# Token mixing: the bias rows of decay and rate as a 65th row of the raising products

## The chip, the cores and the metric

One Trainium2 chip, one of its NeuronCores. The metric is the device time of one execution in microseconds (us), lower is better. TensorE multiplies, VectorE (DVE), ScalarE (ACT) and GpSimd (POOL) do the rest, SyncE (SP) issues most transfers.

## The reference, cut to what matters

The program is a chain of layers over 256 tokens of width 2048. The change lies in the first of them, in the token mixing (an RWKV-7 recurrence with 16 heads of 64). Of its 288 narrow columns the first 64 raise the decay, the next 64 the rate `a`, the last 160 the gate:

```
r, k, v, zw, za, zg = _split(z, RW_SPLITS)          # ..., 64, 64, 160 columns
w_log = -jax.nn.softplus(-(w0 + jnp.tanh(zw) @ w_decay_up).astype(f32)) - 0.5
decay = jnp.exp(-jnp.exp(w_log))
a = jax.nn.sigmoid((a0 + za @ w_icl_up).astype(f32))
g = jax.nn.sigmoid(zg) @ w_gate_up
```

`w_decay_up` and `w_icl_up` are 64 x 1024, `w_gate_up` is 160 x 1024, `w0` and `a0` are rows of 1024. After this come the recurrence over the tokens, an attention branch, an expert layer and two more layers, which the change doesn't touch.

## The kernel before, in words

All weights come as one stream of units of 128 x 2048 values (1 MB). A unit lands in one of four slots (`ring`), ACT writes its rounded part (`hi_w`, lines 216 and 217), DVE the rest (`lo_w`, lines 222 and 224), and TensorE multiplies: line 635 (`quarter`) issues six products of 128 x 512 for a quarter of a unit, 24 for a unit. SP loads the unit four ahead when TensorE has finished one.

Everything else in this stage is laid by hand between the quarters of that stream. The token mixing is done in four pieces `n` = 0 to 3 (two halves of 512 columns, `hf`, times two tiles of 128 tokens, `i`), and `due(u, g, o)` says at which unit `u` and quarter `g` a step of a piece stands: piece `n` begins at unit 35.25 + 12 `n`, and step `o` stands `o` units later. Every engine walks the same table in its own order, and semaphores hold them together. For one piece:

- `ups` (o = 0, lines 775 to 778): the raising of decay and rate. Line 775 multiplies a row of ones (partition 32 of `zgT2`) by the row `w0` (partition 32 of `gup2`), line 776 adds the product of `zT[0:64]` (turned columns of the decay) and `up[0:64]`; lines 777 and 778 do it for the rate with partition 64 and partitions 64 to 127. They are plain float32, and each such product is two instructions on TensorE in the trace.
- `sigmoids` (ACT, lines 1104 and 1105) turn both banks into `sg` and `aa`, `rates` (DVE) uses `aa`.
- `sums` (o = 1, lines 789 to 793): three products of `sg` with masks of 128 x 128, and eight tiny ones.
- then `turns`, `levels`, a solve on DVE with round trips through DRAM, `first`, `second` (line 855), `third`, `states` and `reads`, up to o = 11.25, and `chain` (lines 907 and 916) for four chunks at o = 11.5, 11.75, 12 and 12.25. `inflow` (lines 880 and 881) follows in the first three of them. Piece `n` + 1 thus does its `ups` right behind chunk 2 of piece `n`, then comes one quarter of the stream, then chunk 3.

In chunk 0 of pieces 0 and 2 the state is zero; line 913 then closes the sum with a row of zeros (`zgT2[32:33, 1]`) times `gup2[32:33]`. `gates_up` (lines 834 and 835) raises the gate: 128 rows, and the tail of 32 rows at partitions 0 to 31 of `zgT2` and `gup2`.

`turn_z` (lines 756 to 758) turns the 288 columns of both token tiles to partitions, once, ahead of unit 34; ACT copies them out (lines 1217 to 1219), and POOL writes the rows of ones and of zeros (lines 1339 to 1341). SP loads `up`, `w0`, `a0` and the gate's rows for a half at units 21 and 51 (lines 488 to 490) and 21 and 66 (496 and 497).

Of the kernel before, what the change touches and what calls it, by code (L numbers as in the profile page):

```python
# [13 lines left out]
P = 128  # L14
T = 256
NT = T // P
# [12 lines left out]
CH = 32  # L29
# [86 lines left out]
def build(nc, dram, consts):  # L116
# [13 lines left out]
    def S(name):  # L130
        if name not in sems:
            sems[name] = nc.alloc_semaphore(name)
        return sems[name]
# [16 lines left out]
    def sb(name, shape, dt=F32):  # L150
        n = int(np.prod(shape[1:])) * 4
        h = nc.alloc_sbuf_tensor_at(name, tuple(shape), dt, offset=bump[0])
        bump[0] += (n + 31) // 32 * 32
        assert bump[0] <= top, (name, bump[0], top)
        return h

    def over(name, shape, dt, offset):

        return nc.alloc_sbuf_tensor_at(name, tuple(shape), dt, offset=offset)

    PS = nc.alloc_psum_tensor("PS", (P, 8, 512), F32)
# [14 lines left out]
    ident = sb("ident", (P, P))  # L176
# [146 lines left out]
    HC = 512  # L323
# [3 lines left out]
    zs = sb("zs", (P, NT, 288))  # L327
# [8 lines left out]
    def at_(off, name, shape, dt=F32):  # L336
        return over(name, shape, dt, A1 + off)
# [52 lines left out]
    ST0 = at_(36864, "ST0", (P, 4, P))  # L390
    lwlb = at_(38912, "lwlb", (P, 2, HC))
    par = at_(43008, "par", (P, 3, HC))
    up = at_(49152, "up", (P, HC))
    gup1 = at_(51200, "gup1", (P, HC))
    gup2 = at_(53248, "gup2", (P, HC))
    zT = at_(55296, "zT", (P, NT, P))
    zgT = at_(56320, "zgT", (P, NT, P))
    zgT2 = at_(57344, "zgT2", (P, NT, P))
    small = A1 + 58368
    anti = over("anti", (P, P), F32, small)  # L400
    TC = over("TC", (P, NH, 16), F32, small)
# [41 lines left out]
    def state_of(n, c):  # L443

        return rkv_of(n)[1].rearrange("p (q k) -> p q k", q=4) if c % 2 else ST0[:]
# [14 lines left out]
    with nc.Block() as block:  # L460
        @block.sync
        def _(sp):
# [18 lines left out]
            def half_row(name, hf):  # L481
                return dram[name].rearrange("(a n) -> a n", a=1)[:, hf * HC:(hf + 1) * HC]

            def ups(hf):

                if hf:
                    sp.wait_ge(S("up_ps"), 2)
                sp.dma_start(up[:], dram["up"][:, hf * HC:(hf + 1) * HC]).then_inc(S("up_in"), 16)
                sp.dma_start(gup2[32:33, :], half_row("w0", hf)).then_inc(S("up_in"), 16)
                sp.dma_start(gup2[64:65, :], half_row("a0", hf)).then_inc(S("up_in"), 16)  # L490

            def gups(hf):

                if hf:
                    sp.wait_ge(S("gt_ps"), 2)
                sp.dma_start(gup1[:], dram["gate_up"][0:P, hf * HC:(hf + 1) * HC]).then_inc(S("gup_in"), 16)
                sp.dma_start(gup2[0:32, :], dram["gate_up"][P:P + 32, hf * HC:(hf + 1) * HC]).then_inc(S("gup_in"), 16)

            def pars(hf):

# [44 lines left out]
            for c in range(4):  # L545
                cs = slice(c * 512, (c + 1) * 512)
# [58 lines left out]
        def _(t):  # L605
# [144 lines left out]
            def turn_z():  # L750

                t.wait_ge(S("z_act"), 1)
                t.wait_ge(S("qk_read"), 16)
                for tt in range(NT):
                    cs = slice(tt * P, (tt + 1) * P)
                    nc.tensor.transpose(PS[:, 3, cs], zs[:, tt, 0:P], ident[:])
                    nc.tensor.transpose(PS[:, 3, 2 * P + tt * P:3 * P + tt * P], zs[:, tt, P:2 * P], ident[:])
                    m = nc.tensor.transpose(PS[0:32, 4, cs], zs[:, tt, 2 * P:288], ident[:])
                m.then_inc(S("z_ps"), 1)

            mm_ = nc.tensor.matmul

            def ups(n):

                hf, i = divmod(n, 2)
                b = 5 if n == 0 else 4
                t.wait_ge(S("z_T"), 1)
                t.wait_ge(S("up_in"), 48 * (hf + 1))
                t.wait_ge(S("one_row"), 1)
                if n == 0:  # L770
                    t.wait_ge(S("o_T"), 2)
                else:
                    t.wait_ge(S("F_sb"), n)
                    t.wait_ge(S("RW_sb"), n)
                mm_(PS[:, 6, :], zgT2[32:33, 0, :], gup2[32:33, :], start=True, stop=False)
                mm_(PS[:, 6, :], zT[0:64, i, :], up[0:64, :], start=False, stop=True)
                mm_(PS[:, b, :], zgT2[64:65, 0, :], gup2[64:65, :], start=True, stop=False)
                mm_(PS[:, b, :], zT[64:P, i, :], up[64:P, :], start=False, stop=True).then_inc(S("up_ps"), 1)

            def sums(n):  # L780

# [45 lines left out]
            def gates_up(n):  # L827

                hf, i = divmod(n, 2)
                b = 3 if n < 3 else 6  # L830
                t.wait_ge(S("gup_in"), 32 * (hf + 1))
                if n < 3:
                    t.wait_ge(S("LM_sb"), 8 * n + 16)
                mm_(PS[:, b, :], zgT[:, i, :], gup1[:], start=True, stop=False)
                mm_(PS[:, b, :], zgT2[0:32, i, :], gup2[0:32, :], start=False, stop=True).then_inc(S("gt_ps"), 1)

            def first(n):

# [35 lines left out]
            def inflow(n, c):  # L874

                r, v_ = rows[c], rkv_of(n)[2]
                zero = n % 2 == 0 and c == 0
                for h in range(NH):
                    o = PS[half(h), (7, 3)[c % 2], hs[h // 2]]
                    mm_(o, bb[r, hs[h]], WU[r, h, HD:P], start=h < 2, stop=False)  # L880
                    m = mm_(o, Es[r, hs[h]], v_[r, hs[h]], start=False, stop=zero and h >= 6)
                if zero or c == 3:
                    m.then_inc(S("bb_used"), 1)
# [14 lines left out]
            def chain(n, c):  # L898

                t.wait_ge(S("F_sb"), n + 1)  # L900
                t.wait_ge(S("RW_sb"), n + 1)
                if 4 * n + c:
                    t.wait_ge(S("ST_sb"), 4 * n + c)
                zero = n % 2 == 0 and c == 0
                for h in range(NH):
                    if not zero:
                        m = mm_(PS[half(h), (7, 3)[c % 2], hs[h // 2]], FT[half(h), c, h // 2, :], state_of(n, c)[half(h), h // 2, half(h)],
                                start=False, stop=h >= 6)
                if not zero:
                    m.then_inc(S("ch_ps"), 1)  # L910
                r = rows[c]
                if zero:
                    mm_(PS[r, 5, :], zgT2[32:33, 1, 0:CH], gup2[32:33, :], start=False, stop=True)
                for q in range(4):
                    if not zero:
                        m = mm_(PS[r, 5, q * P:(q + 1) * P], RWT[:, q, r], state_of(n, c)[:, q, :], start=False, stop=q == 3)
                if c == 3:
                    m.then_inc(S("Y_ps"), 1)
                else:
                    inflow(n, c + 1)  # L920
# [33 lines left out]
            for u in range(LASTU):  # L954
                b = u - 1
# [65 lines left out]
        def _(a):  # L1021
# [137 lines left out]
            for U in range(1, LASTU + 1):  # L1159
                u = U - 1  # L1160
                m, q = divmod(u, SLOTS)
# [26 lines left out]
                if u in (6, 7):  # L1188
                    i = u - 6
# [15 lines left out]
                if u in (13, 17):  # L1205
                    i = (u - 13) // 4
# [7 lines left out]
                    out_o(1)  # L1214
                if u == 33:
                    a.wait_ge(S("z_ps"), 1)
                    a.copy(zT[:], PS[:, 3, 0:256].rearrange("p (t c) -> p t c", t=NT))
                    a.copy(zgT[:], PS[:, 3, 256:512].rearrange("p (t c) -> p t c", t=NT))
                    a.copy(zgT2[0:32], PS[0:32, 4, 0:256].rearrange("p (t c) -> p t c", t=NT))
                    a.drain().then_inc(S("z_T"), 1)  # L1220
                if u >= WIN + 11 and (u - WIN) % 2:
                    turned_mixed((u - WIN - 11) // 2)
# [15 lines left out]
                if u in (73, 74):  # L1238
# [3 lines left out]
                    k = slice(4 * (u - 73), 4 * (u - 73) + 4)  # L1242
# [40 lines left out]
        def _(g):  # L1283
# [51 lines left out]
            for u in range(LASTU):  # L1335
                m, q = divmod(u, SLOTS)
                if u == 32:
                    g.wait_ge(S("z_ps"), 1)
                    g.memset(zgT2[32:33, 0, :], 1.0)
                    g.memset(zgT2[64:65, 0, :], 1.0)  # L1340
                    g.memset(zgT2[32:33, 1, :], 0.0)
                    g.drain().then_inc(S("one_row"), 1)
                for n in range(4):
                    if u == math.ceil(RB + RSTEP * n + 3.6):
                        steps_in(n)
                        clear(state_of(n, 1), "K_zero")
                    if u == math.ceil(RB + RSTEP * n + 6.5):
                        steps_back(n)
                if q == 3 and 4 <= m <= 10:
                    shift(m)  # L1350
                if q == 3 and 11 <= m < 19:
                    gate_out(m - 11)
                if u == 46:
                    g.wait_ge(S("scaled"), 7)
                    clear(ST0[:], "ST0_zero")
                if u >= WIN and u < WIN + 8 and (u - WIN) % 2:
                    mix_out((u - WIN) // 2)
# [2297 lines left out]
```

## Time and profile before

| | |
|---|---|
| time, median of 3 executions | 3580.5 us (3577.4 to 3585.12) |
| profiled execution, its own time | 3584.5 us |
| its span, first to last instruction | 3582.3 us |
| mean granted TensorE clock | 0.992 of full speed |
| TensorE (PE) busy | 3525.8 us, 98% |
| DVE busy | 2154.5 us, 60% |
| ACT busy | 1751.3 us, 49% |
| POOL busy | 342.4 us, 10% |

Busy is the time in which an engine has an instruction under way. A granted clock of 1 is 2.4 GHz and one of 0.5 is 1.2 GHz. The token mixing with its four pieces lies between 250 and 730 us of the span.

### The profile page before, as it was taken

The page shows a single profiled execution, that of the slowest core. Times are in us where ns is not written, and L with a number is a line of the kernel's source. Part 1 is how long each engine was busy: PE and PEld are TensorE (multiplying, and loading weights), DVE is VectorE, ACT ScalarE, POOL GpSimd, SP SyncE. Part 2 cuts the span into 40 slices and gives each one's busy share as a digit, 9 for nine tenths or more (in the row PEclk, how much of TensorE's full clock was granted, in tenths as well). Part 3 has the DMA queues.
Part 4 walks back from the last instruction along what each step waited for, and adds up shares of the span by engine and source line. Part 5 has one row for each costly group of instructions (what it writes and reads, how often), then busy time and mean ns, then how long its engine had stood idle before and what let it go on. Part 6 is the DMA issues. An engine that isn't in the chain of part 4 may idle for free. (4 is left out here: it accounts for less than half of the span.)

```text
span 3582.3 us, 50784 instructions
## 1 busy us (share of the span) xinstructions
PE 3525.8 (98%) x20442; PEld 2987.8 (83%) x20442; DVE 2154.5 (60%) x2871; ACT 1751.3 (49%) x2611; POOL 342.4 (10%) x217
## 2 busy tenths in 40 slices
PE   8999999999999999999999999999999999999999
PEld 7767777778899999888899998887888877788777
DVE  4877654765577487555544465556688775565454
ACT  5653433333444686444444444445655644444753
POOL 0000000000199300000000000000122210000000
PEclk9999999999999999999999999999999999999999
DMA  6654423465545555555555666554533435455334
GB/s 229 208 181 140 165 88 132 163 235 180 197 176 185 174 177 181 212 187 187 188 211 187 231 232 226 190 188 175 187 133 133 144 135 188 174 195 188 118 141 164
DMA packets 111179, 638.53 MB, mean 178 GB/s; under 512 B 17738, under 2 KB 23658, under 8 KB 39192
## 3 DMA queue, kind: packets, MB, share of 16 engines
q1 hardware_dynamic: 106664, 622.98, 48.8%
q0 software_dynamic: 4336, 13.14, 1.1%
q8 instruction: 116, 1.90, 0.2%
q14 instruction: 63, 0.52, 0.0%
HBM read 611.10 MB, written 21.54 MB: 177 GB/s over the span
## 5 line engine op out<-in xcount | busy, mean ns | idle before, releaser
L222 DVE TENSOR_TENSOR lo_w<-ring,hi_w 128x1024 fp32r<-128x1024 f32 x500 | 612.2, 1224 | 957.2 <-ACT hi_w L216 949.3
L216 ACT CAST hi_w<-ring 128x1024 fp32r<-128x1024 f32 x540 | 568.9, 1054 | 947.0 <-DMA ring<-in_wstream 922.2
L224 DVE TENSOR_TENSOR lo_w<-ring,hi_w 128x1024 fp32r<-128x1024 f32 x500 | 611.7, 1223 | 0.0
L2035 PE MATMUL PS<-hi_x,hi_w 128*128 128x256 f32 x2048 | 579.7, 283 | 3.0 <-POOL lo_w L224 3.0
L2035 PE MATMUL PS<-hi_x,lo_w 128*128 128x256 f32 x2048 | 575.1, 281 | 0.0
L2035 PE MATMUL PS<-lo_x,hi_w 128*128 128x256 f32 x2048 | 569.9, 278 | 0.0
L217 ACT CAST hi_w<-ring 128x1024 fp32r<-128x1024 f32 x540 | 564.8, 1046 | 0.0
L2061 PE MATMUL PS<-hi_w,hi_g 128*128 128x512 f32 x1024 | 404.0, 395 | 1.2 <-issue 1.2
L2061 PE MATMUL PS<-lo_w,hi_g 128*128 128x512 f32 x1024 | 403.5, 394 | 0.0
L2061 PE MATMUL PS<-hi_w,lo_g 128*128 128x512 f32 x1024 | 403.2, 394 | 0.0
L2035 PEld LDWEIGHTS PS<-hi_x,hi_w 128*128 128x128 f32 x2048 | 385.6, 188 | 3.5 <-ACT GG L2275 3.4
L2035 PEld LDWEIGHTS PS<-lo_x,hi_w 128*128 128x128 f32 x2048 | 386.7, 189 | 0.1
L2035 PEld LDWEIGHTS PS<-hi_x,lo_w 128*128 128x128 f32 x2048 | 384.5, 188 | 0.0
L635 PE MATMUL PS<-hi_w,hi_x 128*128 128x512 f32 (+2 forms) x760 | 311.0, 409 | 2.8 <-DVE lo_w L224 2.3
L635 PE MATMUL PS<-hi_w,lo_x 128*128 128x512 f32 (+2 forms) x760 | 298.6, 393 | 0.0
L635 PE MATMUL PS<-lo_w,hi_x 128*128 128x512 f32 (+2 forms) x760 | 295.5, 389 | 0.0
L2643 PE MATMUL PS<-hi_w,hi_x 128*128 128x512 f32 x616 | 248.6, 404 | 8.4 <-DVE hq L2985 2.7
L2643 PE MATMUL PS<-hi_w,lo_x 128*128 128x512 f32 x616 | 245.5, 398 | 0.0
L2643 PE MATMUL PS<-lo_w,hi_x 128*128 128x512 f32 x616 | 241.6, 392 | 0.0
L2275 ACT ACTIVATE GG<-PS 128x256 f32<-128x256 f32 x128 | 81.3, 637 | 323.9 <-PE PS L2035 321.7
L2061 PEld LDWEIGHTS PS<-hi_w,hi_g 128*128 128x128 f32 x1024 | 192.7, 188 | 45.7 <-issue 1.3
L2061 PEld LDWEIGHTS PS<-hi_w,lo_g 128*128 128x128 f32 x1024 | 192.1, 188 | 45.7
(580 smaller groups left out, 5736.4 us busy)
## 6 DMA issues: line engine op xcount, KB each, us to landing
ring<-in_wstream SPq DMA_DIRECT2D x540, 1024.0 KB, 4.8
other_G<-staged SPq DMA_DIRECT2D x32, 256.0 KB, 6.1
hot<-other_G SPq DMA_DIRECT2D x8, 1024.0 KB, 6.9
gates_dram<-gst POOLq DMA_DIRECT2D x8, 512.0 KB, 4.6
x_dram<-x SPq DMA_DIRECT2D x2, 2048.0 KB, 11.4
x<-x_dram SPq DMA_DIRECT2D x2, 2048.0 KB, 9.6
prev<-RKV POOLq DMA_DIRECT2D x6, 508.0 KB, 5.4
x<-in_x SPq DMA_DIRECT2D x4, 512.0 KB, 8.9
```

The costliest lines, as they stand in the source:

```text
L216: a.copy(hi_w[s][:, 0:HALF], ring[s][:, 0:HALF]).then_inc(S(f"hi{s}"), 1)
L217: a.copy(hi_w[s][:, HALF:UNIT], ring[s][:, HALF:UNIT]).then_inc(S(f"hi{s}"), 1)
L222: v.tensor_tensor(lo_w[s][:, 0:HALF], ring[s][:, 0:HALF], hi_w[s][:, 0:HALF].bitcast(F32), ALU.subtract)
L224: v.tensor_tensor(lo_w[s][:, HALF:UNIT], ring[s][:, HALF:UNIT], hi_w[s][:, HALF:UNIT].bitcast(F32), ALU.subtract)\
L635: mm = nc.tensor.matmul(PS[:, bank(m, tt), 0:n], xa[:, xo + kk_, tt * P:(tt + 1) * P], wa[slot][:, k * 512:k * 512 + n], start=(kk_ == 0 a ...
L2035: m = nc.tensor.matmul(PS[:, s, 0:T], wa[s][:, k * P:(k + 1) * P], xa[:, k, :], start=(k == 0 and p == 0), stop=(k == KC - 1 and p == 2))
L2061: m = nc.tensor.matmul(PS[:, 4 * tt + c, :], ga[:, s, tt * P:(tt + 1) * P], wa[s][:, c * 512:(c + 1) * 512], start=first and p == 0, stop= ...
L2275: a.activation(gg(i), PS[:, i % SLOTS, 0:T], ACT.Gelu).then_inc(S("gelu_free"), 1)
L2643: mm = nc.tensor.matmul(o, xa[:, kk, tt * P:(tt + 1) * P], wa[q][:, k * 512:(k + 1) * 512], start=(kk == 0 and p == 0), stop=(kk == KC - 1 ...
```

## The change

The two bias rows become a 65th row of their weights, and a row of ones the 65th row of the turned columns, so each of the two sums of `ups` is one product over 65 rows. For that both sets of 64 columns stand at partitions 0 to 63: `turn_z` makes four transposes for a token tile instead of three, with 64 columns in two of them. The gate's tail of 32 moves to partitions 96 to 127 of the same tiles. `gup2` and `zgT2` are gone; the row of zeros of line 913 is now taken from the unit matrix.

```diff
-    up = at_(49152, "up", (P, HC))
-    gup1 = at_(51200, "gup1", (P, HC))
-    gup2 = at_(53248, "gup2", (P, HC))
-    zT = at_(55296, "zT", (P, NT, P))
-    zgT = at_(56320, "zgT", (P, NT, P))
-    zgT2 = at_(57344, "zgT2", (P, NT, P))
+    up = at_(49152, "up", (P, 2, HC))
+    gup1 = at_(53248, "gup1", (P, HC))
+    zT = at_(55296, "zT", (P, 2, NT, P))
+    zgT = at_(57344, "zgT", (P, NT, P))
+    UPK, TAIL = slice(0, 65), slice(96, P)
...
-                sp.dma_start(up[:], dram["up"][:, hf * HC:(hf + 1) * HC]).then_inc(S("up_in"), 16)
-                sp.dma_start(gup2[32:33, :], half_row("w0", hf)).then_inc(S("up_in"), 16)
-                sp.dma_start(gup2[64:65, :], half_row("a0", hf)).then_inc(S("up_in"), 16)
+                for k, name in enumerate(("w0", "a0")):
+                    sp.dma_start(up[0:64, k, :], dram["up"][64 * k:64 * k + 64, hf * HC:(hf + 1) * HC]).then_inc(S("up_in"), 16)
+                    sp.dma_start(up[64:65, k, :], half_row(name, hf)).then_inc(S("up_in"), 16)
...
-                sp.dma_start(gup2[0:32, :], dram["gate_up"][P:P + 32, hf * HC:(hf + 1) * HC]).then_inc(S("gup_in"), 16)
+                sp.dma_start(up[TAIL, 0, :], dram["gate_up"][P:P + 32, hf * HC:(hf + 1) * HC]).then_inc(S("gup_in"), 16)
...
-                    nc.tensor.transpose(PS[:, 3, cs], zs[:, tt, 0:P], ident[:])
-                    nc.tensor.transpose(PS[:, 3, 2 * P + tt * P:3 * P + tt * P], zs[:, tt, P:2 * P], ident[:])
-                    m = nc.tensor.transpose(PS[0:32, 4, cs], zs[:, tt, 2 * P:288], ident[:])
+                    gs = slice(2 * P + tt * P, 3 * P + tt * P)
+                    nc.tensor.transpose(PS[:, 3, gs], zs[:, tt, P:2 * P], ident[:])
+                    nc.tensor.transpose(PS[0:64, 3, cs], zs[:, tt, 0:64], ident[:])
+                    nc.tensor.transpose(PS[0:64, 4, cs], zs[:, tt, 64:P], ident[:])
+                    m = nc.tensor.transpose(PS[:, 4, gs], zs[:, tt, 288 - P:288], ident[:])
...
-                t.wait_ge(S("up_in"), 48 * (hf + 1))
+                t.wait_ge(S("up_in"), 64 * (hf + 1))
...
-                mm_(PS[:, 6, :], zgT2[32:33, 0, :], gup2[32:33, :], start=True, stop=False)
-                mm_(PS[:, 6, :], zT[0:64, i, :], up[0:64, :], start=False, stop=True)
-                mm_(PS[:, b, :], zgT2[64:65, 0, :], gup2[64:65, :], start=True, stop=False)
-                mm_(PS[:, b, :], zT[64:P, i, :], up[64:P, :], start=False, stop=True).then_inc(S("up_ps"), 1)
+                mm_(PS[:, 6, :], zT[UPK, 0, i, :], up[UPK, 0, :], start=True, stop=True)
+                mm_(PS[:, b, :], zT[UPK, 1, i, :], up[UPK, 1, :], start=True, stop=True).then_inc(S("up_ps"), 1)
...
-                mm_(PS[:, b, :], zgT2[0:32, i, :], gup2[0:32, :], start=False, stop=True).then_inc(S("gt_ps"), 1)
+                mm_(PS[:, b, :], zT[TAIL, 0, i, :], up[TAIL, 0, :], start=False, stop=True).then_inc(S("gt_ps"), 1)
...
-                    mm_(PS[r, 5, :], zgT2[32:33, 1, 0:CH], gup2[32:33, :], start=False, stop=True)
+                    mm_(PS[r, 5, :], ident[64:65, 0:CH], up[64:65, 0, :], start=False, stop=True)
...
-                    a.copy(zT[:], PS[:, 3, 0:256].rearrange("p (t c) -> p t c", t=NT))
+                    a.copy(zT[0:64], PS[0:64, 3:5, 0:256].rearrange("p k (t c) -> p k t c", t=NT))
                     a.copy(zgT[:], PS[:, 3, 256:512].rearrange("p (t c) -> p t c", t=NT))
-                    a.copy(zgT2[0:32], PS[0:32, 4, 0:256].rearrange("p (t c) -> p t c", t=NT))
+                    a.copy(zT[TAIL, 0], PS[TAIL, 4, 256:512].rearrange("p (t c) -> p t c", t=NT))
...
-                    g.memset(zgT2[32:33, 0, :], 1.0)
-                    g.memset(zgT2[64:65, 0, :], 1.0)
-                    g.memset(zgT2[32:33, 1, :], 0.0)
+                    g.memset(zT[64:65], 1.0)
```

The order of TensorE's instructions around the `ups` of piece 1, in the kernel before: the end of `inflow` of piece 0 (880, 881), the four products, and the first of the stream. Sizes are those of the result.

```order
L880 MATMUL PS<-WU,bb 64x64
L881 MATMUL PS<-RKV,Es 64x64
L775 MATMUL PS<-gup_127,zgT_130 128x512
L776 MATMUL PS<-up,zT 128x512
L777 MATMUL PS<-gup_127,zgT_130 128x512
L778 MATMUL PS<-up,zT 128x512
L635 MATMUL PS<-hi_w_60,hi_x 128x512
```

The same place in the changed kernel, where line numbers are one lower or so:

```order
L879 MATMUL PS<-WU,bb 64x64
L880 MATMUL PS<-RKV,Es 64x64
L776 MATMUL PS<-up,zT 128x512
L777 MATMUL PS<-up,zT 128x512
L634 MATMUL PS<-hi_w_60,hi_x 128x512
L634 MATMUL PS<-lo_w_52,hi_x 128x512
```

Two products have gone and nothing around them has moved. The second place is TensorE at `turn_z`, before:

```order
L733 MATMUL PS<-ident,pn 128x128 x4
L756 MATMUL PS<-ident,zs 128x128
L757 MATMUL PS<-ident,zs 128x128
L758 MATMUL PS<-ident,zs 32x128
L756 MATMUL PS<-ident,zs 128x128
```

And the change's:

```order
L732 MATMUL PS<-ident,pn 128x128 x4
L756 MATMUL PS<-ident,zs 128x128
L757 MATMUL PS<-ident,zs 64x128
L758 MATMUL PS<-ident,zs 64x128
L759 MATMUL PS<-ident,zs 128x128
L756 MATMUL PS<-ident,zs 128x128
```

One transpose more stands there for each of the two token tiles.

## Rows read from the trace of the kernel before

**Rows 1.** The page's busy time: us, share of the span, instructions.

```profile
PE 3525.8 (98%) x20442; PEld 2987.8 (83%) x20442; DVE 2154.5 (60%) x2871; ACT 1751.3 (49%) x2611; POOL 342.4 (10%) x217
```

**Rows 2.** Timeline of TensorE at `ups` of piece 0: start, us, instructions.

```profile
250.84 1.12 PE L775 MATMUL PS<-gup,zgT 1*128 1x512 f32 x2
251.89 1.12 PE L776 MATMUL PS<-up,zT 64*128 64x512 f32 x2
252.94 1.65 PE L777 MATMUL PS<-gup,zgT 1*128 1x512 f32 x2
254.53 2.07 PE L778 MATMUL PS<-up,zT 64*128 64x512 f32 x2
256.53 0.79 PE L635 MATMUL PS<-hi_w,hi_x 128*128 128x512 f32 x1
...
260.40 0.39 PE L635 MATMUL PS<-hi_w,hi_x 128*128 128x512 f32 x1
```

**Rows 3.** Stretches: length, busy time of each engine, granted clock, DMA.

```profile
253.40:260.20 6.80, 6.80 (x13) 3.40 (x12) 3.61 (x5) 1.25 (x3) 0.51 (x1) 0.50 0.04 14
...
335.30:342.10 6.80, 6.02 (x22) 5.56 (x23) 2.79 (x9) 0.81 (x1) 0.00 (x0) 0.50 0.01 2
454.80:458.20 3.40, 3.40 (x17) 3.40 (x17) 0.00 (x0) 0.00 (x0) 0.00 (x0) 0.50 0.02 5
707.40:714.20 6.80, 6.80 (x38) 5.61 (x38) 0.00 (x0) 0.24 (x1) 0.00 (x0) 0.50 0.01 2
```

**Rows 4.** Timeline of TensorE: `ups` of pieces 1 to 3, and stream after chunk 3.

```profile
367.47 1.12 PE L775 MATMUL PS<-gup,zgT 1*128 1x512 f32 x2
...
378.03 0.49 PE L635 MATMUL PS<-hi_w,hi_x 128*128 128x512 f32 x1
...
485.97 1.12 PE L775 MATMUL PS<-gup,zgT 1*128 1x512 f32 x2
...
496.43 0.50 PE L635 MATMUL PS<-hi_w,hi_x 128*128 128x512 f32 x1
...
604.87 1.12 PE L775 MATMUL PS<-gup,zgT 1*128 1x512 f32 x2
...
615.36 0.50 PE L635 MATMUL PS<-hi_w,hi_x 128*128 128x512 f32 x1
```

**Rows 5.** Timeline of TensorE: `sums` of piece 1.

```profile
382.31 1.02 PE L789 MATMUL PS<-sg,incl 128*128 128x512 f32 x2
383.17 1.02 PE L790 MATMUL PS<-sg,incl 128*128 128x512 f32 x2
...
384.98 0.23 PE L793 MATMUL PS<-chunk,sg 128*64 128x4 f32 x2
```

**Rows 6.** Timeline of TensorE: a quarter and a chunk at full clock.

```profile
600.55 0.50 PE L635 MATMUL PS<-hi_w,hi_x 128*128 128x512 f32 x1
600.89 0.39 PE L635 MATMUL PS<-lo_w,hi_x 128*128 128x512 f32 x1
...
602.14 0.68 PE L907 MATMUL PS<-ST,FT 64*64 64x64 f32 x16
...
603.74 0.34 PE L880 MATMUL PS<-WU,bb 32*64 32x64 f32 x4
```

**Rows 7.** Timeline of TensorE at `turn_z`.

```profile
242.34 0.27 PE L756 MATMUL PS<-ident,zs 128*128 128x128 f32 x1
242.45 0.27 PE L757 MATMUL PS<-ident,zs 128*128 128x128 f32 x1
```

**Rows 8.** Timeline of ACT and DVE, in brackets the idle time before and its releaser.

```profile
249.36 1.01 ACT L1084 COPY oT<-PS 128x1024 f32<-128x1024 f32 x1 [3.17 <-PE PS L746]
...
296.50 1.27 ACT L1032 ACTIVATE RKV<-PS,rstat 128x512 f32<-128x512 f32 x2 [5.04 <-PE PS L635]
...
298.96 1.22 DVE L222 TENSOR_TENSOR lo_w<-ring,hi_w 128x1024 fp32r<-128x1024 f32 x1 [4.67 <-ACT hi_w L216]
```

**Rows 9.** Waits of TensorE from 200 to 760 us: total, times, longest.

```profile
PE PS L855 <- issue: 17.5, 4, 5.2
```

## The prediction

> **What bounds the kernel now.** I read the page first: TensorE has an instruction under way for 98% of the span, the next engine for 60% [rows 1]. So time taken out of TensorE's own list shortens the run unless a wait takes it back. Then I read TensorE's timeline at the first `ups`. Lines 775, 776 and 777 start 1.05 us apart, though two of them have a single row to contract and one has 64. From 777 on the pace changes: 778 starts 1.59 us later and the stream 2.00 us after that [rows 2]. The stretches say why: the granted clock is 0.50, which is 1.2 GHz, from 253.4 to 260.2 us, with TensorE busy throughout [rows 3]. Stepping through the whole span in stretches of 1 us, I find eight low-clock stretches in the token mixing: four begin inside the four `ups` (at 253.4, 369.5, 488.9 and 608.4 us, 6.8 us each; the first stands in [rows 3]), three in the waits ahead of `second`, one at 707.4 us in small products, with no wait near it. Last I read the waits: between 200 and 760 us TensorE's one large wait is that of `second`, 17.5 us in four [rows 9].
>
> **The change part by part.** I count each piece as one block, from the start of `ups` to the point where clock and order are ordinary again.
>
> Before: piece 0 takes from 250.84 to 260.40, 9.56 us, for `ups` and nine stream products [rows 2]. Pieces 1 to 3 take from `ups` to the stream product behind chunk 3 10.56, 10.46 and 10.49 us [rows 4], for `ups`, one quarter and one chunk. The sum is 41.07 us.
>
> After, at full clock: `ups` is two products. A float32 product over 128 rows costs 0.86 us where the next has the same height, and three of them with the step to the next kind take 384.98 - 382.31 = 2.67 us [rows 5]; two thus take 2.67 - 0.86 = 1.81. The quarter takes 1.59 (600.55 to 602.14), the chunk without its `inflow` 1.60 (to 603.74) [rows 6]. Pieces 1 to 3: 1.81 + 1.59 + 1.60 = 5.00 each. Piece 0: 1.81, one stream product of 0.34 and eight of 0.23 (five with the step to the chunk take 1.25) [rows 6]: 4.0. The sum is 19.0 us, and 41.07 - 19.0 = 22.1 us come out.
>
> Of these 22.1 the products themselves are 4 x (4 x 1.05 - 1.81) = 9.6; the other 12.5 are the half clock. That split matters, because the two halves rest on different reasons.
>
> The bounds. The 65-row product has no row. From below I take the 128-row product at 0.86, from above the product of 64 rows at 1.05 as in `ups` [rows 2, 5]; the latter makes the gain 4 x 2 x 0.19 = 1.5 us less. I take 0.86: what 1-row and 64-row products share in this trace is a height of 64 or less, and 65 is past it. A gain beyond that has no reason: the 512 columns are streamed in any case. For the clock the bounds are 0 and 12.5 us. I take the whole: `sums` puts 2.6 us of 128-row float32 products and eight tiny ones in a row and no low stretch begins there in four pieces, and the new `ups` has 1.8 us where the old one has over 4. The low clock began 2.6, 2.0, 2.9 and 3.5 us after the starts of the four `ups` [rows 2 to 4]; the new one is over by 1.8.
>
> A rule speaks against this change, and a row answers it. The four products stand on different rows of the array: 32, 0 to 63, 64, 64 to 127. If such products ran side by side, the bias rows would cost nothing now. They start 1.05 us apart at full clock [rows 2]. By the rows, taking two away is worth 9.6 us; if they did run side by side, the sum would be 12.5 us at most, and nothing if the two wider products had shared the array too. The Trainium skill, page TensorEngine Tiling (Array Packing), section Key Properties, says that tiles work independently and in parallel, and that changing the tiling mode drains the array. The trace shows the second (1.05 against 0.86 us) and not the first.
>
> The moved and added work. `turn_z` gets two transposes more, of 0.11 us each start to start [rows 7], on TensorE's path: -0.2 us of the gain. ACT's copy of `zT` reads 64 x 512 instead of 128 x 256; twice the columns may add about as much again as such a copy takes, 0.2 to 0.4 us. ACT then waits 3.17 us for TensorE's line 746 [rows 8], so it is hidden; without that wait it would push line 1084 by as much. POOL writes one row of 512 instead of three of 128, a unit ahead of its use and with nothing behind it. SP issues four transfers instead of three for a half, with the same bytes, 14 units ahead of use; the unit's transfer behind them leaves later by the issue of one transfer, four units ahead of its own use. The gate's tail and the row of zeros keep their number of rows and columns, only their partitions differ: nothing. `ups` waits for the same producers as before.
>
> What is late next: ACT's sigmoids. In pieces 1 to 3 they follow chunk 3 on ACT, and the distance from chunk 3 to `sums` stays, one chunk and three quarters: both ends move together. In piece 0 four quarters lie between `ups` and `sums`, 24 products of 0.23 us, 5.6 us, now all at full clock; ACT has two sigmoids to do in that, and were it late by a microsecond, it would cost that once. Further down the list, DVE and ACT are held by TensorE: ACT waits 5.04 us for it at 296.50, DVE then 4.67 us for ACT [rows 8], so the chain that ends in the wait of `second` starts from TensorE and moves with it. I take that wait as unchanged, 17.5 us.
>
> The sum: 22.1 - 0.2 = 21.9 us off the profiled execution's own time, 3584.5 (span 3582.3, and 2.2 around it), gives 3562.6. That execution lies 4.0 above the median of the runs shown, 3580.5; from the median it would be 3558.6. The four low stretches at `ups` all had 6.8 us in the profiled run, while that at 454.8 had 3.4 [rows 3], so part of the excess of 4.0 may be what comes out. I predict between the two: **3560 us**.
>
> **The rivals.** (1) The clock still falls. The new `ups` follows `inflow`, small products of 32 rows, in pieces 1 to 3, and at 707.4 us the clock fell behind `reads` and its `inflow` with no `ups` near [rows 3]. If it falls in all four, the gain is 9.6 - 0.2, up to 5 more as the stretch reaches over less work: 3566 to 3571. Against it: full-height products make most of the new block. The Trainium skill, page TensorE: Matmul & The Clock Gate, Part 1, ties the low clock to idle time. In these rows TensorE was busy for 6.80 of 6.80 us [rows 3] and the clock was low, so the trace differs. By that rule the four low stretches would have nothing to do with `ups` and would stay, which is this rival's sum.
>
> (2) The wait of `second` takes part of it. The solve runs through DRAM and DVE; if it depended on time and not on TensorE, each wait of 4 to 5 us would grow by up to 5.5. For it: that wait is there in each piece [rows 9]. Against it: the waits of ACT and DVE for TensorE between `ups` and it [rows 8]. Half of the gain kept: 3570.
>
> (3) Slower, by the same wait taken to its end. If nothing of the solve moved, all 22 us would return as idle time, and the low clock in the wait, 6.8 us at 335.3 [rows 3], would last one such step longer: up to 3.4 us low, 1.7 lost, in each of four, 3580.5 + 7 = 3587. It decides only from the point where the solve keeps over nine tenths of its old time. Nothing in [rows 8] allows that.
>
> (4) The change does not do what it says: a 65-row product priced like two of the old ones, 2.1 us, and with it the low clock: no change, 3580. No row speaks for it.
>
> **How the numbers follow.** Forecast as summed 0.66, rival 1 0.19, rival 2 0.08, rival 4 0.04, rival 3 0.03. The forecast's own range is 3554 to 3566: 1.5 for the 65-row product, and low stretches at the waits of `second` that come out 3.4 or 6.8 us long (1.7 us each way for each of four). With rival 1 and most of rival 2 the range is 3552 to 3571. No change that can be told is within 0.2%, 7 us: 3573 to 3588. Faster 0.93 (forecast, rival 1, rival 2), same 0.04, slower 0.03.
>
> **What would show it.** The two products of `ups` start 0.86 us apart and the stream 0.95 later; no low stretch begins within 4 us of an `ups`; the mean clock goes from 0.992 to about 0.996; piece 1 takes 5.0 us from `ups` to the stream behind chunk 3; `second` still waits 4 to 5 us. I am wrong if a low stretch begins behind chunk 2, if the 65-row products are 1.05 or more apart, or if the waits of `second` sum to over 22 us.

## The result, and the profile of the changed kernel

The changed kernel took 3562.5 us (median of 4 executions, 3561.4 to 3566.7) where the kernel before took 3582.8 (4 executions, 3577.4 to 3585.2). The ratio is 0.9944, with a 95% interval of 0.9931 to 0.9957. A second time (5 executions, beside 15 of the kernel before) it took 3558.8 against 3583.2, ratio 0.9928 (0.9914 to 0.9941). The span of the profiled execution went from 3582.3 to 3560.7 us, 21.6 less, and its mean granted clock from 0.992 to 0.995. The forecast was 3560.

The page's busy times, as in [rows 1]: us, share of the span, instructions.

```profile
PE 3504.2 (98%) x20428; PEld 2981.5 (84%) x20428; DVE 2154.4 (61%) x2871; ACT 1750.9 (49%) x2611; POOL 342.1 (10%) x215
```

TensorE is busy 21.6 us less, as much as the span has lost, and no other engine moved by more than 0.5. So all of the gain is TensorE's own time.

TensorE's timeline at the `ups` of pieces 0 and 1, where [rows 2] and [rows 4] stood: start, us, instructions.

```profile
250.24 1.02 PE L776 MATMUL PS<-up,zT 65*128 65x512 f32 x2
251.10 1.02 PE L777 MATMUL PS<-up,zT 65*128 65x512 f32 x2
251.56 0.80 PE L634 MATMUL PS<-hi_w,hi_x 128*128 128x512 f32 x1
252.19 0.39 PE L634 MATMUL PS<-lo_w,hi_x 128*128 128x512 f32 x1
...
254.05 0.40 PE L634 MATMUL PS<-hi_w,hi_x 128*128 128x512 f32 x1
...
360.54 1.12 PE L776 MATMUL PS<-up,zT 65*128 65x512 f32 x2
361.50 1.02 PE L777 MATMUL PS<-up,zT 65*128 65x512 f32 x2
361.96 0.79 PE L634 MATMUL PS<-hi_w,hi_x 128*128 128x512 f32 x1
...
365.44 0.50 PE L634 MATMUL PS<-hi_w,hi_x 128*128 128x512 f32 x1
```

The two 65-row products start 0.86 us apart in piece 0 and 0.96 in piece 1. The first product of the stream starts 0.46 later and takes 0.63 until the next instead of 0.34, so it overlaps the last of `ups`. The blocks of the prediction are 254.05 - 250.24 = 3.81 us for piece 0 (before 9.56) and 365.44 - 360.54 = 4.90 for piece 1 (before 10.56); pieces 2 and 3 take 4.89 and 4.90. The sum is 18.5 us, against 41.07.

Stretches of the changed kernel: from and to, length, busy time of each engine (PE, PEld, DVE, ACT, POOL), granted clock, DMA.

```profile
250.20:254.20 4.00, 4.00 (x15) 2.60 (x14) 3.26 (x3) 3.93 (x5) 0.00 (x0) 1.00 0.69 283
254.20:262.00 7.80, 7.80 (x43) 5.21 (x42) 4.76 (x6) 5.53 (x8) 1.54 (x3) 1.00 0.58 192
326.80:333.60 6.80, 3.77 (x17) 3.80 (x18) 2.93 (x4) 3.07 (x4) 0.00 (x0) 0.50 0.02 4
360.50:365.50 5.00, 5.00 (x38) 3.21 (x35) 0.00 (x0) 0.84 (x3) 0.00 (x0) 1.00 0.01 3
365.50:373.00 7.50, 7.50 (x42) 4.97 (x41) 4.11 (x5) 7.20 (x9) 0.76 (x1) 1.00 0.43 151
472.90:485.00 12.10, 12.10 (x69) 7.83 (x69) 3.78 (x5) 7.71 (x11) 0.72 (x1) 1.00 0.27 88
587.60:600.00 12.40, 12.40 (x79) 8.07 (x75) 3.97 (x5) 7.91 (x11) 0.72 (x1) 1.00 0.25 89
```

The clock is 1.00 from each `ups` to seven microseconds and more behind it, where [rows 3] has 0.50. What is left of the low clock in the token mixing begins at 326.8, 442.9, 555.5 and 668.2 us, once in each piece: 20.4 us in all, and 20.4 us outside `ups` before. In the profile of the second time no low stretch begins at an `ups` either.

The wait of `second`, as in [rows 9], and the first three transposes of `turn_z`, as in [rows 7].

```profile
PE PS L854 <- issue: 17.2, 4, 5.5
```

```profile
241.62 0.27 PE L756 MATMUL PS<-ident,zs 128*128 128x128 f32 x1
241.73 0.27 PE L757 MATMUL PS<-ident,zs 128*64 128x128 f32 x1
241.84 0.27 PE L758 MATMUL PS<-ident,zs 128*64 128x128 f32 x1
```

The wait is 17.2 us in four (before 17.5): it moved with TensorE. A transpose costs 0.11.

### The profile page after: what moved, and what is told of

The parts are those of the page before. It is cut to its first block and busy times, and to the rows that moved or that the text cites. A ratio compares the mean times of both kernels' runs of the same rounds, so it can differ in the third digit from the quotient of the medians.

```text
span 3560.7 us, 50756 instructions
## 1 busy us (share of the span) xinstructions
PE 3504.2 (98%) x20428; PEld 2981.5 (84%) x20428; DVE 2154.4 (61%) x2871; ACT 1750.9 (49%) x2611; POOL 342.1 (10%) x215
```

## The experiments

Each run below has its own runs of the kernel before beside it, whose medians lie between 3583.1 and 3584.4. "Low at `ups`" means a stretch at a granted clock of 0.50 that begins inside one of the four `ups` or within 4.2 us of its start, in the profiled execution. The question is which part of the old `ups` gave what: two products fewer, the lower clock, or the layout.

**1. Four products over 65 rows.** The changed kernel with each of the two issued twice.

```diff
+                mm_(PS[:, 6, :], zT[UPK, 0, i, :], up[UPK, 0, :], start=True, stop=True)
+                mm_(PS[:, b, :], zT[UPK, 1, i, :], up[UPK, 1, :], start=True, stop=True)
                 mm_(PS[:, 6, :], zT[UPK, 0, i, :], up[UPK, 0, :], start=True, stop=True)
                 mm_(PS[:, b, :], zT[UPK, 1, i, :], up[UPK, 1, :], start=True, stop=True).then_inc(S("up_ps"), 1)
```

> The changed kernel, but each of the two 65-row products of ups is issued twice (the second overwrites the first), so that the float32 work of ups again lasts over 3 us, all of it 65 rows high. Theory A (the low clock comes from products of few rows): no low stretch at ups; each piece 1.7 us longer than in the change, the run 4 x 1.7 = 6.8 us over the change's 3562.5: 3569. Rival B (the low clock comes from the length of a float32 block between stream products, whatever its height): four low stretches return, another 8 to 12 us: 3577 to 3582.

3571.0 us, ratio 0.9965 (0.9952 to 0.9979). The four start 0.86 us apart in piece 0. Its stretches from each `ups` on:

```profile
250.80:258.00 7.20, 7.20 (x26) 4.57 (x25) 5.67 (x6) 3.90 (x5) 0.52 (x1) 1.00 0.40 164
362.30:372.30 10.00, 10.00 (x54) 6.67 (x54) 0.86 (x2) 4.00 (x7) 0.00 (x0) 1.00 0.01 2
477.30:487.30 10.00, 10.00 (x55) 6.64 (x53) 0.81 (x2) 3.94 (x7) 0.00 (x0) 1.00 0.01 2
593.30:604.00 10.70, 10.70 (x59) 7.22 (x57) 1.47 (x3) 4.67 (x8) 0.00 (x0) 1.00 0.02 2
```

The clock stays up at all four `ups`; the four products take 3.03 us in piece 0 and 3.14 in the others. The number of products is not what lowers it.

**2. The one-row products put back.** The changed kernel with a product over one row ahead of each 65-row product, which overwrites it.

```diff
+                mm_(PS[:, 6, :], zT[64:65, 0, 0, :], up[64:65, 0, :], start=True, stop=True)
                 mm_(PS[:, 6, :], zT[UPK, 0, i, :], up[UPK, 0, :], start=True, stop=True)
+                mm_(PS[:, b, :], zT[64:65, 1, 0, :], up[64:65, 1, :], start=True, stop=True)
```

> The changed kernel with two products of one row (512 columns) put back, one ahead of each 65-row product, which overwrites it. Both theories: the two cost 1.05 us each, 2.1 for a piece, 8.4 in all: 3571 without low clock. Theory A says that the low clock may return in some pieces, since half of the block is one row high, and then up to 3576; rival B says that it returns in all four, 3580.

3580.5 us, ratio 0.999 (0.998 to 1.0): the gain is all but gone. Low at all four `ups`:

```profile
254.40:261.20 6.80, 6.80 (x13) 4.14 (x13) 3.37 (x5) 1.09 (x2) 0.52 (x1) 0.50 0.01 3
370.40:377.20 6.80, 6.80 (x32) 4.41 (x32) 0.00 (x0) 1.07 (x3) 0.00 (x0) 0.50 0.00 0
489.90:493.30 3.40, 3.40 (x21) 2.36 (x21) 0.00 (x0) 0.00 (x0) 0.00 (x0) 0.50 0.00 0
605.90:612.70 6.80, 6.80 (x32) 4.41 (x32) 0.00 (x0) 1.09 (x3) 0.00 (x0) 0.50 0.00 0
```

**3. The layout alone.** The changed kernel with four products over 1, 64, 1 and 64 rows, as before the change, from the new places.

```diff
+                mm_(PS[:, 6, :], zT[64:65, 0, 0, :], up[64:65, 0, :], start=True, stop=False)
-                mm_(PS[:, 6, :], zT[UPK, 0, i, :], up[UPK, 0, :], start=True, stop=True)
+                mm_(PS[:, 6, :], zT[0:64, 0, i, :], up[0:64, 0, :], start=False, stop=True)
...
```

> The change's layout, transposes, transfers, copies and memset, but ups as before in four products (1 row, 64 rows, 1 row, 64 rows). If the whole gain is in ups, as the prediction has it, this is the kernel before plus 0.2 us of transposes: 3581 to 3583, the same to what can be measured, with four low stretches of 3.4 to 6.8 us at ups. If the layout is worth something by itself, it is faster or slower than that by more than 7 us.

3582.0 us, ratio 0.9993 (0.9983 to 1.0003). The clock falls at three of the four `ups`, as before in all. The transposes, the four transfers and the new places cost or bring nothing that can be measured.

**4. The kernel before without its one-row products.**

```diff
-                mm_(PS[:, 6, :], zgT2[32:33, 0, :], gup2[32:33, :], start=True, stop=False)
-                mm_(PS[:, 6, :], zT[0:64, i, :], up[0:64, :], start=False, stop=True)
-                mm_(PS[:, b, :], zgT2[64:65, 0, :], gup2[64:65, :], start=True, stop=False)
-                mm_(PS[:, b, :], zT[64:P, i, :], up[64:P, :], start=False, stop=True).then_inc(S("up_ps"), 1)
+                mm_(PS[:, 6, :], zT[0:64, i, :], up[0:64, :], start=True, stop=True)
+                mm_(PS[:, b, :], zT[64:P, i, :], up[64:P, :], start=True, stop=True).then_inc(S("up_ps"), 1)
```

> The kernel before without the two one-row products (the biases w0 and a0 are left out of the sums); the two products of 64 rows stay. They take 2.1 us for a piece. Theory A with a share: 2.1 us of half height is less than the old 4.2 us, so few or no low stretches: 8.4 + 9 to 12.5 us under before, 3562 to 3565. Rival B': any product of 64 rows or less in ups pulls the clock down: 3572 to 3575.

3561.9 us, ratio 0.9936 (0.9915 to 0.9957). No low clock at `ups`. The time is as expected, the price of `ups` is not:

```profile
251.30 0.69 PE L775 MATMUL PS<-up,zT 64*128 64x512 f32 x1
251.31 0.69 PE L776 MATMUL PS<-up,zT 64*128 64x512 f32 x1
251.84 0.59 PE L775 MATMUL PS<-up,zT 64*128 64x512 f32 x1
251.84 0.59 PE L776 MATMUL PS<-up,zT 64*128 64x512 f32 x1
252.36 0.50 PE L635 MATMUL PS<-hi_w,hi_x 128*128 128x512 f32 x1
```

Each product is two instructions, and those of lines 775 and 776 start 0.01 us apart: rows 0 to 63 and rows 64 to 127 of the array work at once. `ups` takes 1.06 us, not the expected 2.1. This contradicts a sentence of the prediction, and two later runs go after it.

**5. The rate's two products a quarter later.** The kernel before with lines 777 and 778 moved behind the next quarter of the stream; nothing is left out.

```diff
                 mm_(PS[:, 6, :], zT[0:64, i, :], up[0:64, :], start=False, stop=True)
+
+            def ups_rate(n):
...
                 mm_(PS[:, b, :], zgT2[64:65, 0, :], gup2[64:65, :], start=True, stop=False)
...
+                    for n in due(u, g, 0.25):
+                        ups_rate(n)
```

> The kernel before with the rate's two products (1 row and 64 rows) one quarter of the stream later than the decay's. No work is removed. Theory A with a share (the clock falls when low products fill a stretch): the 4.2 us are cut in two of 2.1, the low stretches at ups go away or get fewer, up to 12.5 us faster: 3570 to 3576. If the number of low products counts and not their density: same as before, 3583.

3575.0 us, ratio 0.998 (0.997 to 0.9991). One low stretch is left at `ups`, in piece 2 (its first two lines on TensorE, and the stretch):

```profile
479.01 1.12 PE L775 MATMUL PS<-gup,zgT 1*128 1x512 f32 x2
480.06 2.07 PE L776 MATMUL PS<-up,zT 64*128 64x512 f32 x2
...
480.10:486.90 6.80, 6.80 (x30) 3.99 (x30) 0.00 (x0) 0.73 (x2) 0.00 (x0) 0.50 0.00 0
```

With the same four products, three of four falls are gone when other work stands between the pairs: six wide products in piece 0, six and chunk 3 in the others (chunk 3 comes ahead of the rate's pair there). That is worth about 8 us. The fall that is left begins 1.1 us behind the first product, when a single one-row product has run.

**6. The same four products in another order.** The kernel before with both one-row products first, then both 64-row products. The two of each pair then have the same height and stand on different rows and banks.

```diff
                 mm_(PS[:, 6, :], zgT2[32:33, 0, :], gup2[32:33, :], start=True, stop=False)
-                mm_(PS[:, 6, :], zT[0:64, i, :], up[0:64, :], start=False, stop=True)
                 mm_(PS[:, b, :], zgT2[64:65, 0, :], gup2[64:65, :], start=True, stop=False)
+                mm_(PS[:, 6, :], zT[0:64, i, :], up[0:64, :], start=False, stop=True)
```

> The kernel before with the four products of ups reordered, both one-row products first (rows 32 and 64), then both of 64 rows (0 to 63 and 64 to 127), neighbours in different rows and different banks. If products in different rows of the array ran side by side, the pair of 64 rows would start within 0.3 us of each other. By the rows of before they don't: 1.05 us apart again, and the time is that of before, 3580 to 3585.

One execution took 3565.6 us, 14 below the least that I expected: the expectation was wrong. The same kernel again:

> The reordered kernel of side_by_side once more, timed. Its first profile had both pairs start 0.01 us apart and 3565.6 us. If that was no chance: 3563 to 3569, at ups 2.1 us instead of 4.2 for a piece, and a low stretch in some of the four pieces, since the block is still low in rows; 1 to 8 us over the change's 3559 to 3562.5.

3563.7 us against 3584.3, ratio 0.9942 (0.9927 to 0.9956). Its timeline at piece 0 (line 775 and 776 over one row, 777 and 778 over 64):

```profile
251.06 0.69 PE L775 MATMUL PS<-gup,zgT 1*128 1x512 f32 x1
251.07 0.69 PE L776 MATMUL PS<-gup,zgT 1*128 1x512 f32 x1
...
252.12 0.69 PE L777 MATMUL PS<-up,zT 64*128 64x512 f32 x1
252.13 0.69 PE L778 MATMUL PS<-up,zT 64*128 64x512 f32 x1
...
253.18 0.50 PE L635 MATMUL PS<-hi_w,hi_x 128*128 128x512 f32 x1
```

Both pairs run together, and `ups` takes 253.18 - 251.06 = 2.12 us where [rows 2] had over 4. Exchanging two lines brings nearly what the whole change brings: the interval takes in the change's 0.9944 and 0.9928. In both profiled executions two low stretches of 3.4 us remain at `ups`, pieces 1 and 3.

**7. The changed kernel cut to 64 rows.** Both products take rows 0 to 63, so they have the same height and the same rows.

```diff
-                mm_(PS[:, 6, :], zT[UPK, 0, i, :], up[UPK, 0, :], start=True, stop=True)
-                mm_(PS[:, b, :], zT[UPK, 1, i, :], up[UPK, 1, :], start=True, stop=True).then_inc(S("up_ps"), 1)
+                mm_(PS[:, 6, :], zT[0:64, 0, i, :], up[0:64, 0, :], start=True, stop=True)
+                mm_(PS[:, b, :], zT[0:64, 1, i, :], up[0:64, 1, :], start=True, stop=True).then_inc(S("up_ps"), 1)
```

> The changed kernel with the products of ups cut from 65 to 64 rows (the biases are left out of the sums), both in rows 0 to 63. Theory: 64 rows is the lower height, where a product's weights aren't loaded ahead, so 1.05 us each, and as both stand in the same rows they can't run side by side: 2.1 us a piece against 1.8 in the change, 4 x 0.3 us longer: 3560 to 3566, no or few low stretches. If the pair does start together although it shares its rows, ups takes 1.05 and the run is 3 us faster than the change. If the time of a product goes by its rows, 64 is no dearer than 65.

3560.4 us, ratio 0.993 (0.9913 to 0.9948).

```profile
251.56 1.12 PE L776 MATMUL PS<-up,zT 64*128 64x512 f32 x2
252.53 1.02 PE L777 MATMUL PS<-up,zT 64*128 64x512 f32 x2
253.47 0.51 PE L634 MATMUL PS<-hi_w,hi_x 128*128 128x512 f32 x1
```

They run one after the other, 0.97 us apart: the same height on the same rows is not enough. The clock stays up. The weight loads (PEld) of these two products, and below them those of lines 776 and 777 of the kernel before:

```profile
251.56 0.29 PEld L776 LDWEIGHTS PS<-up,zT 64*128 64x128 f32 x2 [0.36 <-issue]
252.10 0.19 PEld L777 LDWEIGHTS PS<-up,zT 64*128 64x128 f32 x1 [0.24 <-issue]
...
251.89 0.29 PEld L776 LDWEIGHTS PS<-up,zT 64*128 64x128 f32 x2 [0.76 <-issue]
252.94 0.18 PEld L777 LDWEIGHTS PS<-gup,zgT 1*128 1x128 f32 x1 [0.76 <-issue]
```

The expectation's theory was that weights of a 64-row product aren't loaded ahead. They are: those of line 777 start at 252.10, the product at 252.53. Where the height changes, the load starts with its product, as at 251.56 here and at 251.89 and 252.94 in the kernel before. So the height by itself isn't what made a product 1.05 us long; the expected 2.1 us for `ups` were 1.91.

**8. Four products over 64 rows, and one-row products in a row.** Two kernels ask which few-row products draw the clock down. The first is experiment 7 with each product issued twice. The second is the changed kernel with both one-row products of experiment 2 ahead, in the order 1, 1, 65, 65.

```diff
+                mm_(PS[:, 6, :], zT[64:65, 0, 0, :], up[64:65, 0, :], start=True, stop=True)
+                mm_(PS[:, b, :], zT[64:65, 1, 0, :], up[64:65, 1, :], start=True, stop=True)
                 mm_(PS[:, 6, :], zT[UPK, 0, i, :], up[UPK, 0, :], start=True, stop=True)
```

> The changed kernel, with each product of the raising cut to the 64 rows 0 to 63 and issued twice: four products over 64 rows, all in the same rows, none over 1 row. The biases are left out of the sums. It asks which few-row products pull the clock down. Theory A (it takes products that use half the array or less, one after the other, for about four microseconds): the four start about 0.97 us apart, some 3.9 us in all, and low stretches begin at the raising in at least two of the four pieces; time 3575 to 3583. Rival B (it takes the products over a single row, or the alternation of heights): no low stretch within 4 us of the raising; time 3567 to 3573, as with the four products over 65 rows, 3571.0.

3569.0 us, ratio 0.9965 (0.9951 to 0.9979): rival B. The four products take 3.6 us at half the array's height, and the clock stays at 1.00. The timeline of piece 0:

```profile
250.67 1.12 PE L776 MATMUL PS<-up,zT 64*128 64x512 f32 x2
251.63 1.02 PE L777 MATMUL PS<-up,zT 64*128 64x512 f32 x2
252.49 1.02 PE L778 MATMUL PS<-up,zT 64*128 64x512 f32 x2
253.34 1.02 PE L779 MATMUL PS<-up,zT 64*128 64x512 f32 x2
254.29 0.50 PE L634 MATMUL PS<-hi_w,hi_x 128*128 128x512 f32 x1
```

> The changed kernel with two products over a single row put ahead of its two products over 65 rows, both in the same row, so that the heights change twice and not four times: 1, 1, 65, 65. With the alternating order 1, 65, 1, 65 the time was 3580.5 and the clock fell at all four raisings. Theory A (time spent in one-row products counts, wherever they stand): the clock falls at least at two of the four raisings, time 3572 to 3581. Rival B (the alternation is what counts): no low stretch at the raisings, starts about 0.97, 0.97 and 0.95 us apart, time 3567 to 3571.

3578.0 us, ratio 0.9978 (0.9968 to 0.9988): theory A. Low at three of four `ups`, with TensorE busy throughout, though this `ups` at full clock is shorter (3.33 us in piece 0 against 3.62) and two of its four products are tall:

```profile
364.30:371.10 6.80, 6.80 (x12) 3.17 (x10) 0.00 (x0) 0.00 (x0) 0.00 (x0) 0.50 0.01 2
487.20:490.60 3.40, 3.40 (x8) 1.98 (x6) 0.00 (x0) 0.00 (x0) 0.00 (x0) 0.51 0.00 0
603.20:606.60 3.40, 3.40 (x8) 1.90 (x6) 0.00 (x0) 0.00 (x0) 0.00 (x0) 0.50 0.00 0
```

The changed kernel was also run a second time as it is; its time stands in the section on the result. No low stretch begins at its `ups`.

> The changed kernel, unaltered, in more rounds, for a narrower interval and a second profile with other places of the low stretches: 3559 to 3567, no low stretch that begins in ups.

Put together, by what stands in `ups` (rows of each product in order), with the time that it takes in piece 0:

| `ups` | at once | low at `ups` | its length in piece 0 | ratio |
|---|---|---|---|---|
| 1, 64, 1, 64 (before) | none | 4 of 4, 27.2 us | 5.69 us, half clock in it | 1 |
| 1, 64, 1, 64 (new layout) | none | 3 of 4, 20.4 us | 4.20 us | 0.9993 |
| 1, 65, 1, 65 | none | 4 of 4, 23.8 us | 4.57 us, half clock in it | 0.999 |
| 1, 1, 65, 65 | none | 3 of 4, 13.6 us | 3.33 us | 0.9978 |
| 1, 64, a quarter (and chunk 3), 1, 64 | none | 1 of 4, 6.8 us | 2.10 us and 2.11 us | 0.998 |
| 1+1, 64+64 | both pairs | 2 of 4, 6.8 us | 2.12 us | 0.9942 |
| 65 four times | none | none | 3.03 us | 0.9965 |
| 64 four times | none | none | 3.62 us | 0.9965 |
| 65, 65 (the change) | none | none | 1.32 us | 0.9944, 0.9928 |
| 64, 64, same rows | none | none | 1.91 us | 0.993 |
| 64+64 | the pair | none | 1.06 us | 0.9936 |

## Why the prediction was right, and where its reading failed

**The sum held.** It forecast 22.1 us out of the four blocks; 41.07 - 18.5 = 22.6 came out. Pieces 1 to 3 took 4.89 to 4.90 us against 5.00, piece 0 3.81 against 4.0. The predicted split was 9.6 for the products and 12.5 for the clock. Measured to the second product of the stream, the new `ups` cost 251.10 - 250.24 + 0.46 + 0.63 - 0.34 = 1.61 us in piece 0 and 1.71 in the others. So the products gave 4 x 4.20 - (1.61 + 3 x 1.71) = 10.1, and the clock 22.6 - 10.1 = 12.5. The span shows a little less, 21.6 us against 22.6 - 0.2; the 0.8 us between them were not traced, and executions of one kernel lie further apart than that. The medians moved by 20.3 us, and by 24.4 the second time.

**The low clock at `ups`.** All four falls went, and rival 1 is out. The prediction gave two reasons. The first, that full-height products do not draw the clock down, was right but too narrow: experiments 7 and 8 show that 64-row products do not either, even four in a row. The second, that the new `ups` is over after 1.8 us while the falls began 2.0 us or more behind the start, does not hold: four 65-row products over 3 us draw no fall (experiment 1), and with one-row products falls began 1.1 us (experiment 5) and 1.2 us (experiment 6) behind the start. In every kernel with a fall at `ups` products over one row stand there, 19 falls at 28 `ups` in seven profiles; in the six profiles without them there is none at 24. Experiment 2 brings all four falls back with nothing else changed. The page TensorE: Matmul & The Clock Gate of the Trainium skill, Part 1, ties the low clock to idle time; these falls came with TensorE busy for the whole stretch, so here the measurement decides against that as the only cause.

**The 65-row product.** It was taken at the price of a 128-row product, 0.86 us, and measured 0.86 in piece 0 and 0.96 behind products of 32 rows. The reason for that price was wrong: it took 1.05 us as the price of a height of 64 or less, but 64-row products among their like cost 0.86 too (experiment 8), and 1.05 is what a product costs with a change of height on both sides. That 0.86 came out is partly luck. What 65 rows gain over 64 is at the edges of `ups`: in piece 0 the first 65-row product takes 0.86 behind the stream, the first 64-row product 0.97. What I did not have is its end: the stream came 0.46 us later and not 0.95, and its first product took 0.63 instead of 0.34. Those two nearly cancel, 0.2 us of gain for each piece, and with the 0.1 behind `inflow` pieces 1 to 3 come out 0.1 under the forecast. Rival 4 is out.

**The wait of `second`.** 17.2 us against 17.5, so rivals 2 and 3 are out: between `ups` and the solve DVE and ACT wait for TensorE, and the chain moved with it.

**The moved work.** Two transposes at 0.11 us cost the 0.2 forecast. ACT's copy of `zT` went from 0.37 to 0.58 us, the low end of the estimate, under its wait. Experiment 3 prices the whole layout at nothing.

**The step that failed, though the forecast held,** is a reading that did not enter the sum: "The trace shows the second (1.05 against 0.86 us) and not the first", said of products on different rows of the array that run side by side. It was drawn from rows in which every two neighbours differ in height, 1 and 64. Nor do the four products stand on different rows, as the prediction has it: row 32 of line 775 is one of rows 0 to 63 of line 776, and row 64 of line 777 one of rows 64 to 127 of line 778, and each of these pairs adds up in one bank. Only lines 776 and 777 have rows and banks of their own, and those two, 64 rows and 1, start 1.05 us apart. Where they have the same height and different rows, they start 0.01 us apart (experiments 4 and 6); on the same rows they do not (experiment 7). Both statements that the prediction quotes from the Trainium skill, page TensorEngine Tiling (Array Packing), section Key Properties, agree with these traces: tiles on rows of their own run in parallel, and a change of mode costs time. By the pair of lines 776 and 777 the change of height is enough to keep products apart that could otherwise run at once. The conclusion for the change, that taking two products away pays, stood all the same, since in the old order none ran beside another. But the misreading hid the cheapest way: an exchange of two lines gives 0.9942.

**What stays open.** Why one-row products lower the clock is not settled. TensorE is busy throughout, and no run looks further. Nor is it shown why the clock falls at some `ups` of a kernel and not at others: experiment 6 falls in pieces 1 and 3 alone, and 1, 1, 65, 65 and the layout alone spare piece 0. In pieces 1 to 3 the small products of `inflow` stand right ahead; they stand there in the kernels without a fall too, and piece 0, where the stream stands ahead, fell in two kernels, so they are neither enough nor needed, but whether they help was not tried. Whether the two banks matter to products that run at once wasn't tried alone, nor was an `ups` whose two products with their bias rows would also run at once: with 65 rows each, they don't fit side by side.

## What to carry to other kernels

Fold a bias into the product as one more row: here the 65th row cost nothing that the times can tell (0.9944 and 0.9928 against 0.9936 for two 64-row products without biases, which run at once), while a product of its own for it cost 1.05 us at full clock and, through the clock that it drew down, 12.5 / 8 = 1.6 us more. Where short products must stay, put those of the same height on different rows and in different banks next to each other, and look in the timeline for starts 0.01 us apart. A row that speaks against a rule counts only if the rule's condition was met in it; here heights alternated and rows were shared, and one exchange of two lines would have shown it.

## What the runs showed of the hardware

- With two products over one row, 0.96 to 1.05 us each, beside two of 65 rows TensorE went from 2.4 to 1.2 GHz at four and three of four `ups` while it was busy throughout (experiments 2 and 8); with four over 64 rows, 3.6 us, or four over 65, 3.0 us, at none.
- A change of height costs about 0.10 us for a float32 product of 512 columns: 0.96 us to the next behind a change, 0.86 without one, and 1.05 where the height changes at both ends. 65 rows count as 128 here: in piece 0 of the change the 65-row product right behind the stream takes 0.86. Behind a change the weight load starts with the product, without one it can start 0.43 us ahead of it (252.10 and 252.53, experiment 7).
- A 64-row product has the price of a 128-row one when it stands between others of its height, 0.86 us to the next (experiment 8). Two take 1.91 us one after the other, and 1.06 as a pair.
- Behind a 65-row float32 product the first of the stream starts after 0.46 us and takes 0.63; behind a 64-row one it starts after 0.94 and takes 0.34 to 0.35. The sums, 1.09 and 1.29, differ by 0.2 us.
